# Hymba-style decoder step: all turns of x ahead of the gate columns, the gate columns behind the second weight chunk, and the gate chain behind the scaled copies

## The chip, the cores and the metric

One core of one Trainium2 chip runs the whole step. The metric is the device time of one execution in microseconds, as the median of the runs shown. All data is float32.

## The reference, cut to what matters

256 prompt tokens and 8 sample tokens (264 columns in all) of width 2048 go through one layer: a mixing half (RMSNorm, one combined input projection, mLSTM heads and sliding-window attention, output projection), a mixture of experts, a gated embedding and a final norm. The change lies in the first hundred microseconds, where this is computed:

```python
h = rmsnorm(x, g_mix)                       # x * rsqrt(mean(x^2) + eps) * g
mq, mk, mv, mo, mi, mf, aq, ak, av = split_in(h @ w_in)
i_pre = mi + b_i                            # input gate, one column a head
logf  = log_sigmoid(mf + b_f)               # forget gate, one column a head
F = cumsum(logf); a = i_pre - F; m_t = F + max(m0, cummax(a))
```

mi and mf are 4 columns each of h @ w_in (the gate columns). All the others are projected in groups of 512 columns. F, a and m_t are what the mLSTM stage needs of the gates.

## The kernel before

Every engine has an instruction stream of its own, written out by hand in the order in which it runs; semaphores join them. mix_project (L306) is the first stage. Its parts:

- **Loads.** SyncE's queue (SP) issues x into x_res in two halves of the 2048 columns (L370; turns 0 to 7 need the first, turns 8 to 15 the second), then four weight chunks of 1 MB (load_chunk, L143), each into a slot of its own in raw. A chunk is 512 weight rows by 512 columns; four chunks make a group. A chunk's successor in the same slot is loaded when TensorE has gone through it. Then SP loads chunk 4, waits for the running maximum of the gates (L377), stores it to DRAM and loads it back spread over all partitions (amax_wide, L380), and goes on with chunks 5 and up, and the first three mLSTM states. ScalarE's queue loads the rows of the gains (grows, L458) and the 8 gate columns of w_in (wg, L460), which are 2048 pieces of 32 bytes. GpSimd spreads wg into columns 0 to 3 and 32 to 35 of each block of wg8 (L354), and then raises n_zero.
- **TensorE.** It runs WARM = 14 matmuls on a constant tile (L415), turns the gain rows (L418), and then turns x (turn, L394): for each of 16 blocks k of 128 columns, three transposes into one of six PSUM banks. ScalarE (even k, L465) and VectorE (odd k, L503) copy a bank out, times the gain, to raw_h; turn k waits for the copy of turn k - 6. From turn 4 on each turn is followed by a gate column matmul for block k - 4 (gate_columns, L407: stationary 36 columns of wg8, moving 264 columns of raw_h; a float32 matmul is two instructions in the trace). TensorE waits for n_zero between turn 3 and turn 4 (L422). Then come chunk 0 of group 0 on raw_h (project_chunk, L153, matmul at L160), a broadcast of the inverse root of the mean square (L432), chunk 1, a wait for the gate chain (L435) with small transposes of its results (L439 to L443), chunk 2, a small matmul for the sample decays (L446), and chunk 3. Groups 1 and 2 (chunks 4 to 11) use hT, which is raw_h times the inverse root.
- **ScalarE.** After its copies it sums the squares of two of the three tiles (L469), takes the root (L475), the exponentials and the logarithm of the gate chain (L477 to L485), eight exponentials of the decay matrix (L490), and copies the banks of groups 1 and 2.
- **VectorE.** After its copies it sums the squares of tile 1 (L506, L508), forms r_rows (L518, after n_zero, since core.ones is set before it), copies r_wide (L521), and runs the gate chain: gates, log sigmoid, two scans (L525 to L543), then copies of the small transposes and the sample decays (L545 to L559). Only then come the 16 scaled copies raw_h times r_wide to hT (L564), the decay matrix et from amax_wide (L569, L570), and the copies of group 0's banks times r_wide (L577).

After this stage come attention, mLSTM, the output projection, norm and router (norm_stage, whose 48 transposes are L265), 32 experts with 192 weight loads of 2048 KB, and the tail. Each begins when the one before it has ended on its engines; SP issues the first expert weights at L1476, after the norm.

Of the kernel before, what the change touches and what calls it, by code (L numbers as in the profile page):

```python
# [25 lines left out]
ALU = mybir.AluOpType  # L26
ACT = mybir.ActivationFunctionType
AX = mybir.AxisListType.X

P = 128  # L30
D = 2048
KD = D // P
SEQ, NS = 256, 8
NT = SEQ + NS
TILES = ((0, P), (P, P), (SEQ, NS))
MH, DK = 4, 256
# [20 lines left out]
C_SLOTS = 3  # L57
WARM = 14
NONE = 4096.0
# [121 lines left out]
def bank_done(core, engine, g, j):  # L181

    engine.wait_ge(core.proj_done, 4 * g + j + 1)
# [122 lines left out]
def mix_project(core, w, hT, mixT, pT, m, ctx):  # L306
# [11 lines left out]
    wg = S("wg", [P, KD, 2 * MH])  # L318
    warm = S("warm", [P, 256])
    squares = S("norm_squares", [P, D])  # L320
# [10 lines left out]
    et, cols, col, sg, tab, mend = m["et"], m["cols"], m["col"], m["sg"], m["tab"], m["mend"]  # L331
    names = ("n_consts n_zero n_warm n_x0 n_x1 n_grows n_gcolsT n_gcols n_wg n_turned n_copied_act n_copied_dve n_squares n_square1 "
             "n_mean n_root n_rows n_wideT n_wide n_scaled gates_done m_small m_causal m_lf1 m_lf2 m_arow m_en m_colsT m_cols m_sT m_sg1 m_sg2 m_diag m_tabT "
# [5 lines left out]
    with nc.Block() as block:  # L339
        @block.gpsimd  # L340
        def _(pool):
            link = chain(pool, core.pool_chain)
            nc.gpsimd.memset(warm[:], 1.0).then_inc(q["n_warm"], 1)
            link(nc.gpsimd.memset(core.ident[:], 0.0))
            link(nc.gpsimd.affine_select(out=core.ident[:], in_=core.ident[:], compare_op=ALU.not_equal,
                                         fill=1.0, base=0, pattern=[[-1, P]], channel_multiplier=1))
            link(nc.gpsimd.memset(r[:], 1.0))
            pool.sem_inc(q["n_consts"], 1)
            link(nc.gpsimd.memset(wg8[:], 0.0))
            link(nc.gpsimd.memset(core.ones[:], 1.0))  # L350
            link(nc.gpsimd.memset(core.eps[:], EPS))
            pool.wait_ge(q["n_wg"], 16)
            for b in range(2):
                link(nc.gpsimd.tensor_copy(wg8[:, :, 32 * b:32 * b + MH], wg[:, :, b * MH:(b + 1) * MH]))  # L354
            pool.sem_inc(q["n_zero"], 1)
            link(nc.gpsimd.affine_select(out=core.upper[:], in_=core.ones[:], compare_op=ALU.is_gt,
                                         fill=0.0, base=0, pattern=[[1, P]], channel_multiplier=-1))
            link(nc.gpsimd.memset(causal[:], 0.0))

            link(nc.gpsimd.affine_select(out=causal[:], in_=causal[:], compare_op=ALU.is_ge, fill=-BIG,  # L360
                                         base=0, pattern=[[1, 256]], channel_multiplier=-1))
            pool.sem_inc(q["m_causal"], 1)

        @block.sync
        def _(sp):
# [5 lines left out]
            for n in range(NCH):  # L371
# [3 lines left out]
            sp.dma_start(sg[:, 0, :], w["state_mlstm_m"][0]).then_inc(q["m_small"], 16)  # L375
            load_chunk(core, sp, NCH)
            sp.wait_ge(q["m_arow"], 1)  # L377
            sp.dma_start(core.amax_rows, amax[:]).then_inc(q["m_amax"], 16)
            sp.wait_ge(q["m_amax"], 16)
            sp.dma_start(amax_wide[:].rearrange("p h t -> p (h t)"),  # L380
                         core.amax_rows.rearrange("(o h) t -> o (h t)", o=1).to_broadcast([P, MH * SEQ])
                         ).then_inc(q["m_amax"], 16)
            for n in range(NCH + 1, after + NCH):
                load_chunk(core, sp, n)
                if n == NCH + 1:
                    sp.wait_ge(q["n_squares"], 1)
                    sp.wait_ge(q["n_square1"], 1)
                    sp.wait_ge(q["gates_done"], 1)
                if n - NCH - 1 < C_SLOTS:
                    load_state(core, sp, w, m["cst"], n - NCH - 1)  # L390

        @block.tensor
        def _(pe):
# [12 lines left out]

            def gate_columns(k):  # L407

                pe.wait_ge(q[("n_copied_act", "n_copied_dve")[k % 2]], k // 2 + 1)
                return nc.tensor.matmul(ps[0:32 + MH, 6, 0:NT], wg8[:, k, :], raw_h[:, k, :],  # L410
                                        start=(k == 0), stop=(k == KD - 1))

            pe.wait_ge(q["n_warm"], 1)
# [5 lines left out]
            pe.wait_ge(q["n_x0"], 48)  # L419
            for k in range(4):  # L420
                turn(k)
            pe.wait_ge(q["n_zero"], 1)  # L422
            for k in range(4, KD):
                turn(k)
                gate_columns(k - 4)
            for k in range(KD - 4, KD):
                last = gate_columns(k)
            last.then_inc(q["gates_done"], 1)
            project_chunk(core, pe, raw_h, 0)
            pe.wait_ge(q["n_rows"], 1)  # L430
            for t, (t0, n) in enumerate(TILES):
                last = nc.tensor.matmul(ps[:, 7, t0:t0 + n], r_rows[0:n, t, :], core.ident[0:n, 0:n], start=True, stop=True)  # L432
            last.then_inc(q["n_wideT"], 1)
            project_chunk(core, pe, raw_h, 1)
            pe.wait_ge(q["m_arow"], 3)  # L435
            for kind in range(3):
                for b in range(2):
# [5 lines left out]
            nc.tensor.transpose(ps[0:NS, 7, MH:2 * MH], lf[:, SEQ:NT], core.ident[0:MH, 0:MH]).then_inc(q["m_sT"], 1)  # L443
            project_chunk(core, pe, raw_h, 2)
            pe.wait_ge(q["m_diag"], 1)
            nc.tensor.matmul(ps[:, 6, 0:64], core.ones[0:NS, :], diag[:].rearrange("p a b h -> p (a b h)"),  # L446
                             start=True, stop=True).then_inc(q["m_tabT"], 1)
            project_chunk(core, pe, raw_h, 3)
            for n in range(NCH, after):
                if n == NCH:  # L450
                    pe.wait_ge(q["n_scaled"], KD)
                project_chunk(core, pe, hT, n)

        @block.scalar
        def _(act):
            at = 0
            for name, n in (("g_mix", 16), ("g_mh", 8), ("g_ffn", 16), ("g_ple", 16)):
                act.dma_start(core.grows[at:at + n, :], w[name].rearrange("l (k p) -> (l k) p", p=P)).then_inc(q["n_grows"], 16)  # L458
                at += n
            act.dma_start(wg[:], w["w_in"][0].rearrange("(k p) c -> p k c", p=P)[:, :, C_GATES:C_GATES + 2 * MH]  # L460
                          ).then_inc(q["n_wg"], 16)
            act.wait_ge(q["n_gcols"], 1)
            for k in range(0, KD, 2):
# [31 lines left out]
        def _(dve):  # L495
# [19 lines left out]
            link(V.reciprocal(r[:], r[:]))  # L515
            dve.wait_ge(q["n_zero"], 1)
            for t in range(3):
                ins = V.tensor_scalar(r_rows[:, t, :], core.ones[:], r[:, t:t + 1], None, ALU.mult)  # L518
            ins.then_inc(q["n_rows"], 1)
            dve.wait_ge(q["n_wideT"], 1)  # L520
            link(V.tensor_copy(r_wide[:], ps[:, 7, 0:NT]))  # L521
            dve.wait_ge(q["gates_done"], 1)
            for b in range(2):
# [38 lines left out]

            for k in range(KD):
                V.tensor_tensor(hT[:, k, :], raw_h[:, k, :], r_wide[:], ALU.mult).then_inc(q["n_scaled"], 1)  # L564

            dve.wait_ge(q["m_causal"], 1)
# [6 lines left out]
            link(V.tensor_copy(tab[:, 0:2].rearrange("p a b h -> p (a b h)"), ps[:, 6, 0:64]))  # L573
            for j in range(4):

                bank_done(core, dve, 0, j)
                V.tensor_tensor(pT[:, GROUP_TILES[0] + j, :], ps[:, j, 0:NT], r_wide[:], ALU.mult).then_inc(core.copied["V"], 1)  # L577
            for g in range(1, A_GROUPS):
# [1696 lines left out]
```

## Time and profile before

| | us |
|---|---|
| median of 3 runs (lowest to highest) | 1798.15 (1793.78 to 1799.5) |
| the profiled execution | 1802.88 |
| its span | 1801.2 |
| TensorE busy, weight loads busy | 1413.7 (78%), 809.0 (45%) |
| VectorE, ScalarE, GpSimd busy | 264.1, 305.4, 101.4 |

The span runs from the first to the last instruction of the core. The profile cuts it into 40 slices of 45 us and shows for each how busy an engine was and which clock TensorE was granted (in tenths of full speed), and it lists who waited for whom. Times of instructions are counted from the span's start.

### The profile page before, as it was taken

The numbers are of one execution on the slowest core, as the hardware profiler recorded it, in microseconds if no ns is written. First come the engines' busy times: TensorE is split into PE (matmuls) and PEld (weight loads), VectorE is DVE, ScalarE is ACT, GpSimd is POOL, SyncE is SP. The second block draws the span as 40 slices with busy tenths as digits, with TensorE's granted clock in tenths as the row PEclk, the third lists the DMA queues.
The fourth block names the chain that finished last, engine by engine and source line by source line (L and its number), as shares of the span: only waits on it lengthen the run. The fifth ranks groups of instructions, "written<-read, shape, count | busy, mean of one in ns | idle before, by whom it ended". The sixth has DMA issues, their size and how long they took to land. (4 is left out here: it accounts for less than half of the span.)

```text
span 1801.2 us, 21059 instructions
## 1 busy us (share of the span) xinstructions
PE 1413.7 (78%) x8611; PEld 809.0 (45%) x8612; DVE 264.1 (15%) x725; ACT 305.4 (17%) x560; POOL 101.4 (6%) x190
## 2 busy tenths in 40 slices
PE   7999999999996657666676767677676767676997
PEld 3787888888885532222222222222222222223553
DVE  1402220046514210000000000000000000001312
ACT  1202121132201001111111111111111111112303
POOL 0000000010000011010101010101000010100000
PEclk6999998999998558888878787878777787878999
DMA  4547342469751829999999999999999999973532
GB/s 144 178 160 217 117 127 89 139 252 332 256 213 44 307 99 428 428 426 427 427 428 428 427 427 428 426 423 415 423 412 416 425 412 426 417 323 116 196 135 101
DMA packets 108772, 541.01 MB, mean 300 GB/s; under 512 B 15032, under 2 KB 37756, under 8 KB 82077
## 3 DMA queue, kind: packets, MB, share of 16 engines
q1 hardware_dynamic: 101348, 531.58, 74.3%
q0 software_dynamic: 5200, 8.67, 1.3%
q8 instruction: 34, 0.56, 0.1%
q10 hardware_dynamic: 2176, 0.09, 0.1%
q14 instruction: 14, 0.11, 0.0%
HBM read 523.99 MB, written 24.62 MB: 305 GB/s over the span
## 5 line engine op out<-in xcount | busy, mean ns | idle before, releaser
L1758 PE MATMUL ps<-raw,xT_slots 128*32 128x512 f32 x1536 | 245.0, 770 | 198.7 <-DMA raw<-in_w_gate 95.8
L160 PE MATMUL ps<-hT,raw 128*128 128x264 f32 x1280 | 295.0, 391 | 0.0
L160 PEld LDWEIGHTS ps<-hT,raw 128*128 128x128 f32 x1280 | 243.8, 192 | 43.2 <-issue 1.3
L1778 PE MATMUL ps<-more,hid 128*32 128x512 f32 x1024 | 179.3, 837 | 63.5 <-DMA more<-in_w_down 49.4
L1758 PEld LDWEIGHTS ps<-raw,xT_slots 128*32 128x32 f32 x1536 | 46.8, 123 | 349.3 <-DMA raw<-in_w_up 130.0
L160 PE MATMUL ps<-mixT,raw 128*128 128x264 f32 x640 | 147.4, 391 | 1.2 <-PEq L927 1.2
L1767 PEld LDWEIGHTS ps<-fold,gu 128*128 128x128 f32 x512 | 83.2, 244 | 112.1 <-ACT gu L1679 62.3
L160 PEld LDWEIGHTS ps<-mixT,raw 128*128 128x128 f32 x640 | 122.2, 192 | 23.0 <-issue 2.0
L1991 PE MATMUL ps<-raw,gate_xT 128*128 128x512 f32 x256 | 113.5, 600 | 0.3 <-DMA raw<-in_w_ple_gate 0.3
L1778 PEld LDWEIGHTS ps<-more,hid 128*32 128x32 f32 x1024 | 34.2, 131 | 176.7 <-DMA more<-in_w_down 86.9
L1728 DVE TENSOR_TENSOR hid<-ps,sig 128x128 f32<-128x128 f32 x32 | 9.3, 291 | 699.3 <-PE ps L1767 699.3
L1767 PE MATMUL ps<-fold,gu 128*128 128x32 f32 x512 | 90.7, 328 | 23.1 <-ACT gu L1679 23.1
L1758 PE MATMUL ps<-more,xT_slots 128*32 128x512 f32 x512 | 88.6, 829 | 9.2 <-DMA more<-in_w_up 8.3
L1749 PEld LDWEIGHTS ps<-ident,xe 128*64 128x64 f32 x1056 | 66.3, 216 | 39.2 <-issue 39.2
L1682 ACT ACTIVATE xT_slots<-ps 128x512 f32<-128x512 f32 x32 | 19.1, 597 | 349.3 <-PE ps L1749 336.7
L1749 PE MATMUL ps<-ident,xe 128*64 128x64 f32 x1056 | 70.9, 289 | 5.7 <-DMA xe<-ffn_rows,gi 5.7
L1991 PEld LDWEIGHTS ps<-raw,gate_xT 128*128 128x128 f32 x256 | 48.3, 192 | 57.9 <-issue 57.4
L1852 POOL DMA_INDIRECT expert_rows<-yq,si x32 | 32.9, 1028 | 697.2 <-DVE yq L1736 697.2
L1736 DVE COPY yq<-ps 128x512 f32<-128x512 f32 x32 | 22.1, 691 | 227.2 <-PE ps L1778 227.2
L1673 ACT ACTIVATE gu<-ps 128x512 f32<-128x512 f32 x32 | 19.1, 597 | 200.8 <-PE ps L1758 200.8
L1676 ACT ACT_TABLE_LOAD x32 | 41.1, 1283 | 0.6
L1673 ACT ACT_TABLE_LOAD x32 | 41.1, 1283 | 0.5
(383 smaller groups left out, 892.5 us busy)
## 6 DMA issues: line engine op xcount, KB each, us to landing
raw<-in_w_gate SPq DMA_DIRECT2D x64, 2048.0 KB
more<-in_w_down SPq DMA_DIRECT2D x64, 2048.0 KB, 28.6
raw<-in_w_up SPq DMA_DIRECT2D x32, 2048.0 KB
more<-in_w_up SPq DMA_DIRECT2D x32, 2048.0 KB
raw<-in_w_in SPq DMA_DIRECT2D x44, 1024.0 KB, 5.1
raw<-in_w_out SPq DMA_DIRECT2D x16, 1024.0 KB, 5.9
raw<-in_w_ple_gate SPq DMA_DIRECT2D x16, 1024.0 KB, 5.1
x_res<-in_state_mlstm_C SPq DMA_DIRECT2D x8, 1024.0 KB, 9.6
```

Of the source, the lines that this page charges most:

```text
L160: return nc.tensor.matmul(ps[:, j, 0:NT], core.raw[:, q % NCH, k * GW + j * P:k * GW + (j + 1) * P], xT[:, core.groups[g].k0 + c * CK + k, ...
L1673: nc.scalar.activation(gu[:, 0, :], ps[:, GATE, :], ACT.Copy).then_inc(q["gu_copied"], 1)
L1676: nc.scalar.activation(sig[:], ps[:, GB, 0:4 * SLOTS].rearrange("p (k s) -> p k s", k=4), ACT.Sigmoid).then_inc(q["sig_ready"], 1)
L1682: nc.scalar.activation(xT[:], ps[:, XB, :].rearrange("p (k s) -> p k s", k=EK), ACT.Copy).then_inc(q["x_copied"], 1)
L1728: V.tensor_tensor(hid[:], ps[:, GB, 0:4 * SLOTS].rearrange("p (k s) -> p k s", k=4), sig[:], ALU.mult).then_inc(q["h_step"], 1)
L1736: V.tensor_copy(yq[:], ps[:, YB, :]).then_inc(q["y_copied"], 1)
L1749: last = nc.tensor.matmul(ps[h * 64:(h + 1) * 64, XB, k * 64:(k + 1) * 64], by_row[:, k, :], quarters[:, h], start=True, stop=True)
L1758: last = nc.tensor.matmul(ps[own, (GATE, UP)[m], :], xT[:, k, i * SLOTS:(i + 1) * SLOTS], chunk(m * EI + i)[:, k * GW:(k + 1) * GW], start ...
L1767: last = nc.tensor.matmul(ps[:, GB, (m * 4 + j) * SLOTS:(m * 4 + j + 1) * SLOTS], gu[:, m, :].rearrange("p (i r k) -> p i k r", i=EI, k=2) ...
L1778: last = nc.tensor.matmul(ps[a * SLOTS:(a + 1) * SLOTS, YB, :], hid[:, 2 * i + k, :], chunk(2 * EI + i)[:, k * D + a * GW:k * D + (a + 1) ...
L1852: pool.indirect_dma_start(out=y4, out_offset=bass.IndirectOffsetOnAxis(ap=si[:, 0:1], axis=0), in_=yq[:], in_offset=None, bounds_check=8 * ...
L1991: last = nc.tensor.matmul(ps[:, 2 * t + g % 2, :], xT[:, c * CK + k, t * P:(t + 1) * P], core.raw[:, c, k * GW:(k + 1) * GW], start=(c == ...
```

## The change

- TensorE: 9 warm-up matmuls in place of 14. All 16 turns in one row, without a wait for n_zero and without gate columns between them. One wait for all copies, then chunks 0 and 1, the broadcast of the inverse root, and only then n_zero and the 16 gate column matmuls. Chunks 2 and 3, chunks 4 to 6, the small transposes (with their wait for m_arow), chunk 7, the small matmul of the decays (with its wait for m_diag), and chunks 8 to 11 follow.
- VectorE: r_rows waits for n_ones, raised right behind the memset of core.ones, and no more for n_zero. The scaled copies to hT, and the copies of group 0's banks, stand ahead of the gate chain.
- SP: chunks 4 and up are loaded as slots come free, without a wait between them; the store of amax stands behind the issue of chunk 8, its spread load behind the issue of chunk 9. The states are loaded with chunks 4, 5 and 6.
- ScalarE: one tiny activation (L460 and following) as soon as the warm-up tile is set.

```diff
-WARM = 14
+WARM = 9
@@ gpsimd
             link(nc.gpsimd.memset(core.ones[:], 1.0))
+            pool.sem_inc(q["n_ones"], 1)
@@ sync
-            load_chunk(core, sp, NCH)
-            sp.wait_ge(q["m_arow"], 1)
-            sp.dma_start(core.amax_rows, amax[:]).then_inc(q["m_amax"], 16)
-            sp.wait_ge(q["m_amax"], 16)
-            sp.dma_start(amax_wide[:]...).then_inc(q["m_amax"], 16)
-            for n in range(NCH + 1, after + NCH):
+            for n in range(NCH, after + NCH):
                 load_chunk(core, sp, n)
-                if n == NCH + 1:
+                if n == NCH:
+                    sp.wait_ge(q["n_turned"], KD)
                     sp.wait_ge(q["n_squares"], 1)
                     sp.wait_ge(q["n_square1"], 1)
-                    sp.wait_ge(q["gates_done"], 1)
-                if n - NCH - 1 < C_SLOTS:
-                    load_state(core, sp, w, m["cst"], n - NCH - 1)
+                if n - NCH < C_SLOTS:
+                    load_state(core, sp, w, m["cst"], n - NCH)
+                if n == NCH + 4:
+                    sp.wait_ge(q["m_arow"], 1)
+                    sp.dma_start(core.amax_rows, amax[:]).then_inc(q["m_amax"], 16)
+                if n == NCH + 5:
+                    sp.wait_ge(q["m_amax"], 16)
+                    sp.dma_start(amax_wide[:]...).then_inc(q["m_amax"], 16)
@@ tensor
-            for k in range(4):
+            for k in range(KD):
                 turn(k)
-            pe.wait_ge(q["n_zero"], 1)
-            for k in range(4, KD):
-                turn(k)
-                gate_columns(k - 4)
-            for k in range(KD - 4, KD):
-                last = gate_columns(k)
-            last.then_inc(q["gates_done"], 1)
+            pe.wait_ge(q["n_copied_act"], KD // 2)
+            pe.wait_ge(q["n_copied_dve"], KD // 2)
             project_chunk(core, pe, raw_h, 0)
+            project_chunk(core, pe, raw_h, 1)
             pe.wait_ge(q["n_rows"], 1)
             ...
             last.then_inc(q["n_wideT"], 1)
-            project_chunk(core, pe, raw_h, 1)
+            pe.wait_ge(q["n_zero"], 1)
+            for k in range(KD):
+                last = nc.tensor.matmul(ps[0:32 + MH, 6, 0:NT], wg8[:, k, :], raw_h[:, k, :], start=(k == 0), stop=(k == KD - 1))
+            last.then_inc(q["gates_done"], 1)
+            project_chunk(core, pe, raw_h, 2)
+            project_chunk(core, pe, raw_h, 3)
+            pe.wait_ge(q["n_scaled"], KD)
+            for n in range(NCH, NCH + 3):
+                project_chunk(core, pe, hT, n)
             pe.wait_ge(q["m_arow"], 3)
             ...
-            project_chunk(core, pe, raw_h, 2)
+            project_chunk(core, pe, hT, NCH + 3)
             pe.wait_ge(q["m_diag"], 1)
             ...
-            project_chunk(core, pe, raw_h, 3)
-            for n in range(NCH, after):
-                if n == NCH:
-                    pe.wait_ge(q["n_scaled"], KD)
+            for n in range(NCH + 4, after):
                 project_chunk(core, pe, hT, n)
@@ scalar
+            act.wait_ge(q["n_warm"], 1)
+            nc.scalar.activation(first_use[:], warm[:, 0:1], ACT.Copy)
             act.wait_ge(q["n_gcols"], 1)
@@ vector
-            dve.wait_ge(q["n_zero"], 1)
+            dve.wait_ge(q["n_ones"], 1)
             ...
             link(V.tensor_copy(r_wide[:], ps[:, 7, 0:NT]))
+            for k in range(KD):
+                V.tensor_tensor(hT[:, k, :], raw_h[:, k, :], r_wide[:], ALU.mult).then_inc(q["n_scaled"], 1)
+            for j in range(4):
+                bank_done(core, dve, 0, j)
+                V.tensor_tensor(pT[:, GROUP_TILES[0] + j, :], ps[:, j, 0:NT], r_wide[:], ALU.mult).then_inc(core.copied["V"], 1)
             dve.wait_ge(q["gates_done"], 1)
             ...
-            for k in range(KD):
-                V.tensor_tensor(hT[:, k, :], raw_h[:, k, :], r_wide[:], ALU.mult).then_inc(q["n_scaled"], 1)
             ...
             link(V.tensor_copy(tab[:, 0:2].rearrange("p a b h -> p (a b h)"), ps[:, 6, 0:64]))
-            for j in range(4):
-                bank_done(core, dve, 0, j)
-                V.tensor_tensor(pT[:, GROUP_TILES[0] + j, :], ps[:, j, 0:NT], r_wide[:], ALU.mult).then_inc(core.copied["V"], 1)
```

## Rows read from the trace of the kernel before

**Rows 1.** The page's 40 slices of 45 us: DMA share in tenths.

```profile
DMA  4547342469751829999999999999999999973532
```

**Rows 2.** Stretches: length, busy PE, PEld, DVE, ACT, POOL, clock, DMA share, GB/s.

```profile
7.50:10.90 3.40, 3.40 (x19) 2.25 (x17) 0.71 (x2) 1.18 (x1) 0.00 (x0) 1.00 1.05 357
22.40:45.00 22.60, 22.56 (x62) 8.39 (x63) 3.78 (x7) 5.54 (x9) 1.00 (x3) 0.50 0.00 1
65.50:68.90 3.40, 3.40 (x10) 2.58 (x9) 2.91 (x11) 0.21 (x1) 0.00 (x0) 0.50 0.89 296
580.00:593.20 13.20, 13.18 (x48) 7.43 (x48) 3.03 (x7) 3.12 (x8) 0.00 (x0) 0.50 0.43 164
660.00:1600.00 940.00, 651.65 (x4512) 239.90 (x4512) 39.48 (x93) 145.55 (x188) 77.13 (x126) 0.80 1.00 419
```

**Rows 3.** Timelines of VectorE and ScalarE, and one issue of SP, 9 to 600 us.

```profile
11.24 0.49 DVE L503 TENSOR_SCALAR mixT<-ps,gcols 128x264 f32<-128x264 f32 x1 [0.48 <-PE ps L403]
55.27 0.88 DVE L525 TENSOR_TENSOR gates<-ps,norm_r_wide 4x264 f32<-4x264 f32 x2
63.31 0.28 DVE L543 TENSOR_SCALAR arow<-arow 4x256 f32<-4x256 f32 x1
66.57 5.58 DVE L564 TENSOR_TENSOR hT<-mixT,norm_r_wide 128x264 f32<-128x264 f32 x16
...
9.72 1.28 ACT L465 ACT_TABLE_LOAD   x1 [9.60 <-PE ps L403]
42.22 1.90 ACT L469 ACTIVATE norm_squares<-x_res 128x2048 f32<-128x2048 f32 x1
72.85 2.87 ACT L490 ACTIVATE gain_row<-gain_row,cols 128x256 f32<-128x256 f32 x8 [7.04 <-DVE gain_row L570]
...
598.64 0.94 SPq L1476 DMA_DIRECT2D raw<-in_w_gate x2
```

**Rows 4.** Timeline of TensorE, 0 to 140 us: start, length, line, operation, idle time before.

```profile
1.20 7.71 PE L415 MATMUL ps<-warm 128*128 128x256 f32 x28 [1.20 <-POOL warm L343]
...
9.04 2.16 PE L403 MATMUL ps<-ident,x_res 128*128 128x128 f32 x12
22.44 0.89 PE L403 MATMUL ps<-ident,x_res 128*128 128x128 f32 x3 [11.24 <-POOLq L355]
...
24.29 0.89 PE L403 MATMUL ps<-ident,x_res 128*128 128x128 f32 x3
...
43.58 3.11 PE L410 MATMUL ps<-mixT,wg 128*36 128x264 f32 x10
46.62 7.39 PE L160 MATMUL ps<-mixT,raw 128*128 128x264 f32 x32
53.84 0.92 PE L432 MATMUL ps<-ident,norm_r_rows 128*128 128x128 f32 x6
54.69 7.39 PE L160 MATMUL ps<-mixT,raw 128*128 128x264 f32 x32
63.64 0.53 PE L439 MATMUL ps<-ident,arow 4*128 4x4 f32 x6 [1.56 <-DVE arow L543]
...
64.15 9.07 PE L160 MATMUL ps<-mixT,raw 128*128 128x264 f32 x32
73.16 0.43 PE L446 MATMUL ps<-diag,ones 8*128 8x64 f32 x2
73.52 7.39 PE L160 MATMUL ps<-mixT,raw 128*128 128x264 f32 x32
80.74 57.12 PE L160 MATMUL ps<-hT,raw 128*128 128x264 f32 x256
```

**Rows 5.** Longest waits of GpSimd, 0 to 60 us: total, times, longest.

```profile
POOL wg L354 <- DMA wg<-in_w_in: 18.7, 1, 18.7
```

**Rows 6.** DMA issues in 3.4 to 3.5 us (chunk 0): us to landing last.

```profile
raw<-in_w_in SPq DMA_DIRECT2D x1, 1024.0 KB, 10.5
```

More of the change, by code:

```diff
@@ L318, in mix_project @@
     wg = S("wg", [P, KD, 2 * MH])
-    warm = S("warm", [P, 256])
+    warm, first_use = S("warm", [P, 256]), S("first_use", [P, 1])
     squares = S("norm_squares", [P, D])
@@ L331, in mix_project @@
     et, cols, col, sg, tab, mend = m["et"], m["cols"], m["col"], m["sg"], m["tab"], m["mend"]
-    names = ("n_consts n_zero n_warm n_x0 n_x1 n_grows n_gcolsT n_gcols n_wg n_turned n_copied_act n_copied_dve n_squares n_square1 "
+    names = ("n_consts n_ones n_zero n_warm n_x0 n_x1 n_grows n_gcolsT n_gcols n_wg n_turned n_copied_act n_copied_dve n_squares n_square1 "
              "n_mean n_root n_rows n_wideT n_wide n_scaled gates_done m_small m_causal m_lf1 m_lf2 m_arow m_en m_colsT m_cols m_sT m_sg1 m_sg2 m_diag m_tabT "
@@ L375, in _ @@
             sp.dma_start(sg[:, 0, :], w["state_mlstm_m"][0]).then_inc(q["m_small"], 16)
-            load_chunk(core, sp, NCH)
-            sp.wait_ge(q["m_arow"], 1)
-            sp.dma_start(core.amax_rows, amax[:]).then_inc(q["m_amax"], 16)
-            sp.wait_ge(q["m_amax"], 16)
-            sp.dma_start(amax_wide[:].rearrange("p h t -> p (h t)"),
-                         core.amax_rows.rearrange("(o h) t -> o (h t)", o=1).to_broadcast([P, MH * SEQ])
-                         ).then_inc(q["m_amax"], 16)
-            for n in range(NCH + 1, after + NCH):
+            for n in range(NCH, after + NCH):
                 load_chunk(core, sp, n)
-                if n == NCH + 1:
+                if n == NCH:
+                    sp.wait_ge(q["n_turned"], KD)
                     sp.wait_ge(q["n_squares"], 1)
                     sp.wait_ge(q["n_square1"], 1)
-                    sp.wait_ge(q["gates_done"], 1)
-                if n - NCH - 1 < C_SLOTS:
-                    load_state(core, sp, w, m["cst"], n - NCH - 1)
+                if n - NCH < C_SLOTS:
[5 more added lines that the diff above has]
+                    sp.wait_ge(q["m_amax"], 16)
+                    sp.dma_start(amax_wide[:].rearrange("p h t -> p (h t)"),
+                                 core.amax_rows.rearrange("(o h) t -> o (h t)", o=1).to_broadcast([P, MH * SEQ])
+                                 ).then_inc(q["m_amax"], 16)
         @block.tensor
@@ L405, in turn @@
                 last.then_inc(q["n_turned"], 1)
[L407 to L411, printed above, removed]
             pe.wait_ge(q["n_warm"], 1)
```

## The prediction

> **What bounds the kernel now.** I read the page's slices first. The DMA digits stand at 9 from about 660 us to 1600 us and below that before it [rows 1]: in that stretch the queues run at 419 GB/s with a share of 1.00, and TensorE is busy 652 of 940 us [rows 2]. So the expert stage is bound by its weights. But its first weights are issued at 598.6 us, by an SP that arrives there only when norm and router begin [rows 3]; nothing in it is tied to a fixed time. What comes before is bound by TensorE: from 80.74 us eight chunks follow each other in 57.12 us, 7.14 us each, without a gap [rows 4]. A microsecond saved ahead of chunk 4 should therefore move everything behind it, up to the end.
>
> The timeline of TensorE shows where the first 80 us go [rows 4]. Warm-ups end at 8.9 us; four turns follow in 2.16 us; then TensorE is idle for 11.24 us. The releaser named is GpSimd, and GpSimd itself waited 18.7 us for the 32-byte pieces of wg [rows 5]. When TensorE comes back at 22.44 us its clock is 0.50, that is 1.2 GHz, and stays so to 45 us although it is busy 22.56 of 22.60 us [rows 2]. One turn and one gate column matmul take 24.29 - 22.44 = 1.85 us there. Chunk 0 begins at 46.62 us. Chunks 0 and 1 take 7.2 us each, then TensorE waits 1.56 us for the gate chain, the clock falls again at 65.5 us for 3.4 us, and chunk 2 takes 9.0 us where chunk 3 takes 7.2. **Chunk 4 begins at 80.74 us.** That number is what the change moves.
>
> **The change, part by part.** The sum is the new start of chunk 4.
>
> 1. *Start of the turns.* The second MB of a load behind another follows 3.0 us later at 353 to 357 GB/s (1.05 MB by 0.357) [rows 2]. Chunk 0 landed at 3.4 + 10.5 = 13.9 us [rows 6]; the second half of x, ahead of it, then at about 10.9, and the first at about 7.9. The gain rows had landed by 8.9 us, where TensorE waited for nothing [rows 4]; when, no row shows. Nine warm-ups end between 6.1 and 6.7 us (28 instructions in 7.71 us, at 0.275 us each or less for the ten removed). So the transposes of the gain rows start between 7.9 and 8.9 us; I take 8.2, and the first turn at 8.4. The second half of x is needed by turn 8, which comes after 12.5 us: its wait costs nothing, and at worst (x landing with chunk 0 at 13.9) 1.4 us less what the slower clock already takes.
>
> 2. *Sixteen turns.* At 2.4 GHz four turns took 2.16 us with the tail of the last, 0.52 us each from start to start. At 1.2 GHz the 48 transposes of the later norm took 13.19 us, 0.82 us a turn [rows 2]. There the clock was 0.50 for all 13 us with TensorE busy all the time: turns alone did not bring it up. Whether they let it fall is not shown. From 7.5 to 10.9 us it was kept, with 1.4 us of warm-ups and the four turns in it [rows 2]; in 62 to 65.5 us about as much matmul work, without turns, did not keep it. In the changed kernel the warm-ups are over at 6.7, then comes an idle 1.5 us, then turns alone. I take it that the clock falls near 10.9 us. Then 4.8 turns run in 2.5 us and 11.2 at 0.82 us, 9.2 us: the turns end at 20.1 us. The bounds are 16 x 0.52 = 8.3 us (end at 16.7) and 16 x 0.82 = 13.2 us (end at 21.6). The rotation through six banks costs nothing: a copy takes 0.49 us [rows 3], each engine has one per two turns (1.04 us or more). The early tiny activation takes a table load (1.28 us [rows 3]) out of the way of the first copy; turn 6 is 3 us behind turn 0 and covers it either way: zero, and up to 1.3 us where it did not. The last copy and its hand-over add 0.7 us: **chunk 0 starts at 20.8 us.** Both its load and that of chunk 1 (3.0 us later, 16.9 us) are in.
>
> The Trainium skill ("TensorE: Matmul & The Clock Gate", Part 4, PE-mode transpose) says that the full clock doesn't engage in transpose mode. By that rule all sixteen turns would run at 1.2 GHz and end at 21.6 us in place of 20.1, and 18.8 us would be saved in place of 20.3; the later norm agrees (0.50 throughout), the four turns at 9.04 us, still at the full clock, do not.
>
> 3. *The slow start of chunk 0.* The clock came back at 45.0 us only 1.4 us into unmixed matmuls, and in the second case at 68.9 us, 4.8 us after chunk 2 began. I take 3.4 us at half clock, as in 65.5 to 68.9, which costs 1.7 us (chunk 2's excess over chunk 3 was 1.7); bounds 0.7 and 2.4, half of the two times named.
>
> 4. *The work up to chunk 4.* Four chunks at 7.22 us (46.62 to 53.84) are 28.9; the broadcast of the inverse root is 54.69 - 53.84 = 0.85; sixteen gate column matmuls are 32 instructions with 264 moving columns, which at the full clock go at the chunks' rate (32 in 7.22 us): 7.2 us. The bound above is that of the last ten in the trace, 43.58 to 46.62, 0.30 each over a changing clock: 9.7 us. The small transposes and the decay matmul (0.51 and 0.36 us) now come after chunk 4's start; I add 0.9 so that the comparison is fair.
>
> **Sum:** 20.8 + 1.7 + 28.9 + 0.85 + 7.2 + 0.9 = 60.4 us against 80.74. **20.3 us are saved.**
>
> **What is hidden, and by what.** TensorE's wait for r_rows: the squares begin with the last copy; from their start at 42.22 us to the broadcast at 53.84, which had no idle time ahead, are 11.6 us at most; two chunks of 14.4 us cover it. n_zero came at 22.4 us and is asked for after 37 us; gone with the wait is the whole 11.24 us. r_wide and the sixteen scaled copies (5.58 us) run beside gate columns and chunk 2: 21.7 us of cover. Group 0's bank copies follow the banks, as before. The gate chain then starts behind them, at the end of chunk 3, and takes what it took from 55.27 to 63.59, 8.3 us [rows 3], some 9 us with the last bank copy; TensorE asks for it after three chunks, 21.4 us later. The SP wait for m_arow has the loads of chunks 9 to 11 behind it: it ends about 7.5 us into the group, when chunk 8's slot has just come free; a load is needed 21 us after it can start and takes 5 or so. The next things late would be at the change from group 1 to group 2: VectorE needs the transposes (after chunk 6) and then does the decays (from 63.59, the transposes' 0.5 us among it, to 66.57, so 2.5 us without them) and et; ScalarE's eight exponentials run in step with et and end 3.6 us after it began (72.15 to 75.72); its first bank copy must be there when chunk 8 starts. Transposes at 21.9 us of the group, decays at 24.4, exponentials at 28.0, copy (0.4) at 28.4, chunk 8 at 29.5. That cover is **1.1 us only**, and each microsecond more is lost one for one.
>
> **The rivals.**
> A. *Forecast: the clock falls in the turns, 20.3 us saved.* Own range 18.0 (all turns slow and the latest rise) to 22. Chance 0.62.
> B. *The clock holds through the turns.* They end at 16.7, chunk 0 starts at 17.4 at the full clock: 17.4 + 28.9 + 0.85 + 7.2 + 0.9 = 55.3, saved 25.5, in the run's terms 1772.7 us. For it: it was kept from 7.5 to 10.9 us with turns in it. Against: the later norm. Chance 0.18.
> C. *A new wait at the group change.* amax's spread load stands behind chunk 9's load; with its issue at 14.7 us of the group and a landing as long as chunk 0's 10.5 us it would be there at 25.2, 0.8 us after VectorE asks for it; if it takes twice that, et is 11 us late and TensorE loses 10 of the 20 us: saved 10 to 19, 1779 to 1788 us. Against: by then one load of 1 MB stands ahead of it, where chunk 0 had the whole of x ahead. Chance 0.12.
> D. *No gain at the end*, some later stage waiting for something not moved by the stage before: 1798 us. Against it speaks that the loads of experts are issued when SP gets there [rows 3]. Chance 0.04.
> E. *Slower: the clock stays at 1.2 GHz* beyond the turns, through chunks 0 to 3 and the gate columns, whose stationary side is 36 columns. That work is 37 us at 2.4 GHz and twice that at 1.2: 35.3 us more than forecast, 15 us slower than before, 1813 us. It decides from 44 us of low clock on (half of which eats 20.3 + 1.7 us). Against: both times the clock came back within 5 us of dense matmuls [rows 2, 4]. Chance 0.04.
>
> **The numbers.** The profiled execution took 1802.9 us (span 1801.2): 1782.6 after. The median of the runs is 4.7 us lower, 1798.15: **1777.9 us**. Runs of this kernel spread over 5.7 us, so 0.3% (5.4 us) is about what can be told from no change. Range: B's 1772.7 less 2.5 for that spread, 1770, and on the other side the bounds of A with the gate columns at 9.7 us (1783) and the nearer half of C, 1785. Faster by over 0.3% are A, B and C: 0.92. Within: D, 0.04. Slower: E, 0.04.
>
> **What would show it.** Right: no idle time behind turn 3; turns of 0.52 us up to about 11 us and of 0.82 after; chunk 0 at 20 to 22 us; a granted clock of 0.50 ending up to 5 us into it; gate columns in one row of 7.2 us near 38 us; no wait at L435, L446 or at chunk 8; router and experts earlier by the same 20 us. Wrong: turns with waits for copies or for x; a clock of 1.00 from 4 us on (B); a wait of TensorE for ScalarE's copy at chunk 8 (C); a shift that shrinks between chunk 4 and 660 us (D); a clock of 0.50 past 30 us (E).

## The result, and the profile after

| | before | after |
|---|---|---|
| median of the runs shown (lowest to highest) | 1798.83 (1793.78 to 1803.05), 4 runs | 1778.22 (1776.4 to 1782.85), 4 runs |
| the profiled execution, its span | 1802.88, 1801.2 | 1778.48, 1776.8 |

The ratio is 0.9885, 95% interval 0.9866 to 0.9905: 17 to 24 us faster. The forecast was 1777.9. Six more runs of the changed kernel beside eleven of the kernel before gave 0.9891 (0.9871 to 0.9910), 1778.72 against 1800.44. Intervals in brackets behind a ratio are 95% intervals, here and below. The number was met; the road to it was not the one forecast, as the traces show.

The page's DMA slices of the changed kernel, which answer to [rows 1]: the row of nines, 20 slices long, is the same in kind; a slice is now 44.4 us where it was 45.0.

```profile
DMA  7564432679632759999999999999999999974542
```

TensorE's timeline of the changed kernel, 0 to 114 us, to be held against [rows 4] (start, length, line and operation, idle time before):

```profile
1.20 6.93 PE L411 MATMUL ps<-warm 128*128 128x256 f32 x18 [1.20 <-POOL warm L343]
8.80 0.24 PE L414 MATMUL ps<-ident,grows 56*128 56x56 f32 x1 [0.67 <-DMA grows<-in_g_ple]
8.97 8.44 PE L405 MATMUL ps<-ident,x_res 128*128 128x128 f32 x48
18.04 14.48 PE L160 MATMUL ps<-mixT,raw 128*128 128x264 f32 x64 [0.63 <-ACT mixT L464]
32.35 0.92 PE L424 MATMUL ps<-ident,norm_r_rows 128*128 128x128 f32 x6
33.20 7.31 PE L428 MATMUL ps<-mixT,wg 128*36 128x264 f32 x32
40.44 14.51 PE L160 MATMUL ps<-mixT,raw 128*128 128x264 f32 x64
54.79 21.52 PE L160 MATMUL ps<-hT,raw 128*128 128x264 f32 x96
76.24 0.53 PE L439 MATMUL ps<-ident,arow 4*128 4x4 f32 x6
...
76.75 7.39 PE L160 MATMUL ps<-hT,raw 128*128 128x264 f32 x32
84.07 0.43 PE L446 MATMUL ps<-diag,ones 8*128 8x64 f32 x2
84.43 28.75 PE L160 MATMUL ps<-hT,raw 128*128 128x264 f32 x128
```

The 11.24 us of idle time behind turn 3 are gone; the sixteen turns stand in one row of 8.44 us. Chunks 0 and 1, the broadcast, the gate columns and chunks 2 and 3 follow without a gap. There is no idle time ahead of L439 or of L446. Chunk 4 begins at 54.79 us where it began at 80.74: 25.95 us, of which 0.87 us (transposes and decay matmul, now behind it) is only moved. Most of it lies in the turns and gate columns: they took 37.58 us (9.04 to 46.62) and now take 9.07 and 7.24, which is 21.3 us less, 11.24 of it idle time and some 10 slow clock. The wait for the gate chain gives 1.56 and the slow chunk 2 behind it 1.8; the rest is the moved 0.87 and small gaps. The stretch of the turns, with the clock in the third column from the end:

```profile
9.00:17.40 8.40, 8.40 (x49) 5.32 (x48) 3.67 (x8) 3.84 (x9) 0.00 (x0) 1.00 1.09 358
17.40:45.00 27.60, 26.97 (x124) 20.42 (x123) 10.27 (x28) 6.67 (x8) 1.48 (x5) 1.00 0.62 204
```

The clock stays at 1.00 through the turns and behind them (it had risen at 6.85 us, among the warm-ups), where it stood at 0.50 from 22.4 to 45 us [rows 2].

**How a microsecond of the head reaches the end.** I read four moments in every trace: the first matmul on hT (chunk 4), the first transpose of the later norm, SP's first load of expert weights, and the end of the span.

| kernel | chunk 4 | norm | expert weights | span | from weights to end |
|---|---|---|---|---|---|
| before | 80.74 | 580.02 | 598.64 | 1801.2 | 1202.6 |
| before, second trace | 79.42 | 576.62 | 595.56 | 1797.7 | 1202.1 |
| after | 54.79 | 555.47 | 573.96 | 1776.8 | 1202.8 |
| after, second trace | 54.74 | 555.50 | 574.30 | 1776.5 | 1202.2 |
| after, third trace | 55.89 | 554.66 | 573.18 | 1775.9 | 1202.7 |

From the expert weights on, the time is the same to within 0.7 us in these five, and SP's issue moves with the stage ahead of it:

```profile
573.96 0.94 SPq L1474 DMA_DIRECT2D raw<-in_w_gate x2
```

So what is won ahead of chunk 4 is kept: 25.95 us there, 24.55 at the norm (0.87 of the difference is the moved work, the other 0.5 I did not place), 24.4 at the end.

### The profile page after: what moved, and what is told of

The parts are those of the page before. It is cut to its first block and busy times, and to the rows that moved or that the text cites. A ratio compares the mean times of both kernels' runs of the same rounds, so it can differ in the third digit from the quotient of the medians.

```text
span 1776.8 us, 21041 instructions
## 1 busy us (share of the span) xinstructions
PE 1420.2 (80%) x8601; PEld 808.4 (45%) x8602; DVE 264.9 (15%) x725; ACT 305.5 (17%) x561; POOL 101.4 (6%) x190
## 5 line engine op out<-in xcount | busy, mean ns | idle before, releaser
L1756 PE MATMUL ps<-raw,xT_slots 128*32 128x512 f32 x1536 | 256.8, 803 | 198.6 <-DMA raw<-in_w_gate 110.1
L1776 PE MATMUL ps<-more,hid 128*32 128x512 f32 x1024 | 170.7, 798 | 42.0 <-DVE hid L1729 20.5
L1756 PE MATMUL ps<-more,xT_slots 128*32 128x512 f32 x512 | 103.0, 952 | 11.4 <-DMA more<-in_w_up 11.1
L1756 PEld LDWEIGHTS ps<-more,xT_slots 128*32 128x32 f32 x512 | 18.3, 152 | 53.9 <-issue 39.1
```

The costliest lines, as they stand in the source:

```text
L1756: last = nc.tensor.matmul(ps[own, (GATE, UP)[m], :], xT[:, k, i * SLOTS:(i + 1) * SLOTS], chunk(m * EI + i)[:, k * GW:(k + 1) * GW], start ...
L1776: last = nc.tensor.matmul(ps[a * SLOTS:(a + 1) * SLOTS, YB, :], hid[:, 2 * i + k, :], chunk(2 * EI + i)[:, k * D + a * GW:k * D + (a + 1) ...
```

## The experiments

The table's columns for the variants, with the median of their runs (one run where so marked):

| kernel | chunk 4 | norm | span | median | ratio to before |
|---|---|---|---|---|---|
| e2, 14 warm-ups | 56.75 | 555.83 | 1777.2 | 1781.65 | 0.9902 (0.9882 to 0.9921) |
| e3, no warm-up | 62.34 | 566.83 | 1787.3 | 1785.08 | 0.9917 (0.9898 to 0.9937) |
| e5, gate columns ahead of chunk 0 | 61.17 | 560.61 | 1782.4 | 1785.94 | 0.9932 (0.9906 to 0.9958) |
| e6, the turns' order alone | 65.63 | 564.77 | 1788.0 | 1787.64 | 0.9936 (0.9917 to 0.9954) |
| e7, gate chain ahead of the copies | 54.98 | 556.04 | 1780.0 | 1779.37 | 0.9893 (0.9860 to 0.9925) |
| e8, small transposes behind chunk 3 | 64.45 | 571.20 | 1792.0 | 1792.65 | 0.9950 (0.9931 to 0.9970) |
| e9, gaps closed | 52.92 | 554.46 | 1777.7 | 1778.43 | 0.9891 (0.9870 to 0.9911) |
| e10, turns done twice | 73.66 | 573.97 | 1796.6 | 1798.3 (one) | |

### Both kernels once more: e1, e11 and e4

No edit. I wanted to know whether the full clock in the turns was luck.

> The changed kernel once more, unchanged. Its first trace had the clock at 1.00 through all sixteen turns (8.44 us for 48 transposes) and chunk 4 at 54.79 us. Theory 1 (a full clock reached by the warm-ups is kept by turns alone, whatever the moment of the run): again 8.4 to 8.6 us for the 48 transposes, chunk 4 at 54.5 to 56, span 24 to 25 us under the kernel before's. Theory 2 (the forecast's: it depends on when in the execution the chip looks; the first trace was a lucky one): the clock falls to 0.50 among the turns, these take 10 to 13 us, chunk 4 comes at 58 to 61, and the median of many runs is some 20 us below the kernel before, with runs of both kinds some 5 us apart.

> The changed kernel unchanged, for a third trace. Its ten timed runs lie in two bunches, seven at 1776.4 to 1778.9 us and three at 1781.8 to 1783.0. If a fall of the clock makes the upper bunch, a run of it shows one that the first two traces did not have, 3.4 us or more long, somewhere before 560 us; if this run is of the lower bunch, its clock changes are those of the first two, 10.2 us at 266, 3.4 at 300 and 3.4 at 437 us.

> The kernel before once more, for a second trace: is its first 80 us the same each time? Theory 1: clock 0.50 from 14 to 18 us on until about 45, chunk 4 at 79.5 to 82 us, and the spread of its runs (9 us from lowest to highest) comes from the expert stage. Theory 2: chunk 4 moves by more than 3 us from one execution to the next with the moments at which the clock changes.

The second trace of the changed kernel repeats the first: 48 transposes in 8.44 us, chunk 4 at 54.74. The third has the turns at the full clock too, but then a fall. Its stretches, beginning with the turns, columns as above:

```profile
9.00:17.40 8.40, 7.86 (x46) 4.96 (x45) 3.95 (x9) 4.39 (x9) 0.00 (x0) 1.00 1.09 351
17.50:20.80 3.30, 3.30 (x8) 2.58 (x9) 2.42 (x5) 3.25 (x5) 0.00 (x0) 0.50 1.09 356
20.90:33.00 12.10, 12.10 (x56) 10.32 (x55) 1.21 (x5) 2.66 (x3) 1.48 (x5) 1.00 0.51 167
```

Its chunks 0 and 1 took 16.12 us (17.49 us to 33.45 from start to the next start, 15.96) where they took 14.3 in the first: 1.6 us, at 0.50 for some 3.4 us. That is the size of step 3 of the forecast, in one execution of three. The expectation on the two bunches of times was wrong: this run took 1777.63 us, in the lower bunch, and has the fall. What it lacks is a later fall that the first trace has at 437 us (the first line is of the first trace, the second of the third):

```profile
437.00:440.30 3.30, 3.30 (x9) 2.57 (x9) 2.70 (x15) 0.00 (x0) 0.00 (x0) 0.50 0.98 329
437.00:440.30 3.30, 2.90 (x13) 2.58 (x14) 3.30 (x19) 0.00 (x0) 0.00 (x0) 1.00 0.89 241
```

So its chunk 4 comes 1.1 us later than the first trace's and its norm 0.8 us earlier: a fall more in the head and one less behind it cancel in the total. The timed runs of e1 lay at 1777.5 to 1778.9 (four) and at 1781.8 and 1783.0; what separates them I can't say.

The kernel before: its second trace has the clock at 0.50 from 15 to 46 us like the first, but no fall at 65.5, so that chunk 4 comes 1.3 us earlier. It also has the clock at 1.00 in 459 to 466 us, where the first trace has a fall (461.4 to 464.7 us at 0.51). Of the 3.5 us between the two spans, 3.4 are there at the norm already. So theory 1 held for the head, but these two runs do not differ by the expert stage. The runs beside these spread from 1792 to 1804 us, more than the head explains.

### Does the warm-up carry the turns' clock: e2 and e3

```diff
-WARM = 9
+WARM = 14     # e2
+WARM = 0      # e3
```

> The changed kernel with 14 warm-up matmuls as before. In the first trace of the changed kernel 9 warm-ups ended at 8.13 us because the clock rose at 6.85 only, and the gain rows landed 0.67 us later. Theory 1: 14 of them end at 9 to 10.5 us (0.22 us an instruction at the full clock, 0.44 below it), so chunk 0 starts 0.2 to 1.7 us later and the span is up to 1.7 us longer: not told from no change against the changed kernel. Theory 2: the longer warm-up keeps the clock up for longer among the turns: chunk 4 up to 4 us earlier than in runs of the changed kernel whose clock falls, so a median 1 to 4 us lower.

> The changed kernel without any warm-up matmul, so that the clock has nothing but turns to rise by: prices the case on which the forecast rested. If turns alone do not raise the clock (the later norm's 48 transposes ran 13.2 us at 0.50): 48 transposes take 13.2 us, chunk 0 starts at 22 to 23 us with a half clock for another 2 to 5 us, chunk 4 at 60.5 to 62, 6 to 7 us behind the changed kernel's first trace, ratio to the kernel before 0.990 to 0.993. If they do raise it after all: 9 to 11 us for the turns and chunk 4 at 55 to 58.

TensorE's timeline of e3:

```profile
8.90 0.32 PE L414 MATMUL ps<-ident,grows 56*128 56x56 f32 x1 [8.90 <-DMA grows<-in_g_ple]
9.15 13.19 PE L405 MATMUL ps<-ident,x_res 128*128 128x128 f32 x48
22.98 17.09 PE L160 MATMUL ps<-mixT,raw 128*128 128x264 f32 x64 [0.63 <-issue]
```

Without warm-ups 48 transposes take 13.19 us, exactly what the later norm's took in 580 to 593.2 us [rows 2]: turns alone don't raise the clock. Chunks 0 and 1 then take 16.9 us in place of 14.3, and chunk 4 comes 7.6 us late, 0.3 us beyond what I had expected; the median is 6.4 us above the changed kernel's. A warning on the reading: the stretches of this trace give the clock as 1.00 for the turns.

```profile
9.10:22.30 13.20, 13.20 (x49) 7.46 (x48) 3.67 (x8) 4.10 (x9) 0.48 (x2) 1.00 1.03 329
```

The durations contradict that: 0.275 us a transpose in 13.2 us, against 0.176 in the changed kernel's 8.44. Ahead of the first change of clock in a trace the column isn't a measurement. The same goes for the first microseconds of all of them: 18 warm-up instructions took 6.93 us in the changed kernel, 0.39 each, and 28 took 7.71 in the kernel before, 0.28 each, so part of them ran at the lower clock.

e2 is no better than the changed kernel: 14 warm-ups ended at 9.17 us, the turns came 0.33 us later, and this trace too has a fall right behind the turns.

```profile
9.30:17.70 8.40, 8.40 (x49) 5.36 (x48) 3.66 (x8) 3.81 (x9) 0.00 (x0) 1.00 1.11 347
18.30:21.60 3.30, 3.23 (x8) 2.53 (x9) 2.51 (x5) 3.27 (x4) 0.00 (x0) 0.50 1.02 338
```

So five more warm-ups cost a third of a microsecond at the start and did not prevent the fall in this trace. The medians, 1781.65 and 1778.72, are 2.9 us apart with overlapping intervals.

### Are turns able to keep the clock at all: e10

```diff
-                for t, (t0, n) in enumerate(TILES):
+                for t, (t0, n) in 2 * list(enumerate(TILES)):
                     last = nc.tensor.transpose(ps[:, k % 6, t0:t0 + n], ...)
```

> The changed kernel with every transpose of every turn done twice (96 for 48, into the same places): do turns keep the full clock for as long as they last, or had the sixteen been too short for a fall? Theory 1 (turns keep it): 96 transposes take 16.8 to 17.0 us at 1.00 and chunk 4 comes at 63.1 to 63.5. Theory 2 (a fall that is only late): the clock is 0.50 for part of them, they take 18.5 to 25 us, chunk 4 comes at 65 to 73.

```profile
9.30:12.10 2.80, 2.80 (x17) 1.79 (x17) 0.71 (x2) 0.48 (x1) 0.00 (x0) 1.00 1.08 353
12.20:33.70 21.50, 21.50 (x80) 12.27 (x79) 2.95 (x6) 4.39 (x8) 1.49 (x5) 0.50 0.47 152
```

Theory 2, and early: the turns began at 9.22 us at the full clock, and 3 us later it was 0.50 and stayed so for the remaining 21.5 us of transposes (24.58 us for 96; chunk 4 at 73.66, 0.7 beyond the expected range). This is the forecast's case A, in a kernel whose first 3 us of TensorE are those of the changed kernel but for the repeats and a longer wait for the gain rows. So turns neither raise the clock nor hold it safely. In all eight other traces in which sixteen turns ran in one row from a full clock, it was kept to the last of them, and in e9's, where the gain rows stand between them, too. The loss is one trace of one execution, and what decides between losing and keeping it I did not isolate; in the trace that lost it, TensorE had idled 1.69 us ahead of the turns, but in e8 it had idled 1.46 us and the clock was kept.

### How much is the turns' order alone: e6 and e5

e6 is the kernel before with this edit and no other:

```diff
-            for k in range(4):
+            for k in range(KD):
                 turn(k)
             pe.wait_ge(q["n_zero"], 1)
-            for k in range(4, KD):
-                turn(k)
-                gate_columns(k - 4)
-            for k in range(KD - 4, KD):
+            for k in range(KD):
                 last = gate_columns(k)
```

e5 is the changed kernel with the wait for n_zero and the gate columns moved up, between the wait for the copies and chunk 0.

> The kernel before with one thing changed: TensorE does all sixteen turns in a row, then waits for n_zero and does the sixteen gate column matmuls, then chunk 0 and all the rest as before (14 warm-ups, gate chain ahead of the scaled copies, wait for the gate chain behind chunk 1). Turns at 0.52 us end near 18 us; the gate columns start at 22.4 and end at 31 to 36 us by the clock; from chunk 0 to chunk 4 it is 32.4 to 34.1 us as in the two traces of the kernel before. Theory 1: chunk 4 at 64 to 70 us, 11 to 16 us of the some 25 gained, ratio 0.991 to 0.994; the rest is the placing behind chunk 1. Rival (the clock falls in the turns where the gate columns are next): 48 transposes in 10 us or more, chunk 4 at 68 to 72.

> The changed kernel, with the sixteen gate column matmuls and their wait for n_zero put between the turns and chunk 0: all else as changed. The turns end at 17.4 us, n_zero comes at 22.4. Theory 1 (the gain has two parts, turns ahead of the wait and the gate columns behind other work): TensorE idles 4.5 to 5 us behind the turns, the clock falls in or after that, the gate columns take 9 to 14 us in place of 7.2, chunk 4 comes at 61 to 66 us in place of 54.8, and 6 to 11 us of the gain are lost: ratio to the kernel before 0.992 to 0.996. Rival (only the order of the turns matters, since the clock is kept through 5 us of idle time): chunk 4 at 59.5 to 60, at most 5 us lost.

TensorE's timeline of e6:

```profile
9.93 8.44 PE L403 MATMUL ps<-ident,x_res 128*128 128x128 f32 x48
22.29 9.30 PE L410 MATMUL ps<-mixT,wg 128*36 128x264 f32 x32 [3.92 <-POOLq L355]
31.52 7.39 PE L160 MATMUL ps<-mixT,raw 128*128 128x264 f32 x32
...
48.54 0.53 PE L436 MATMUL ps<-ident,arow 4*128 4x4 f32 x6 [1.55 <-DVE arow L540]
...
49.04 9.07 PE L160 MATMUL ps<-mixT,raw 128*128 128x264 f32 x32
...
65.63 29.53 PE L160 MATMUL ps<-hT,raw 128*128 128x264 f32 x132
```

The order of the turns alone moves chunk 4 from 80.74 to 65.63 us: 15.1 of the 25.95 us. It takes the turns out of the wait and out of the low clock, as theory 1 had it. Its turns also began 0.96 us later than the changed kernel's. Three costs remain: 3.92 us of idle time for n_zero, the gate columns slowed to 9.2 us, and the wait for the gate chain with the fall of the clock behind it (1.55 and 1.8 us, chunk 2 taking 9.0 us as before). e5's timeline shows the first two by themselves:

```profile
8.93 8.44 PE L405 MATMUL ps<-ident,x_res 128*128 128x128 f32 x48
22.77 8.93 PE L422 MATMUL ps<-mixT,wg 128*36 128x264 f32 x32 [5.40 <-POOLq L356]
31.63 14.51 PE L160 MATMUL ps<-mixT,raw 128*128 128x264 f32 x64
```

5.40 us idle, less the 0.63 that it has in the changed kernel, and 8.86 in place of 7.24 us for the gate columns (22.77 to 31.63) make 6.4 us, and chunk 4 comes at 61.17, 6.4 us late. That is theory 1, near its lower edge: the loss is above the rival's 5 us, 4.8 us of it idle time and 1.6 us the clock, which stood at 0.50 for the first 3.3 us of the gate columns and at 1.00 after. The median lost 7.2.

### The order on VectorE, and the distance of the small transposes: e7 and e8

e7 puts VectorE's scaled copies and the bank copies of group 0 behind the gate chain's last m_arow; e8 puts TensorE's wait for m_arow and the small transposes from behind chunk 6 to right behind chunk 3.

> The changed kernel with VectorE's gate chain (up to the third m_arow) ahead of the sixteen scaled copies and the four bank copies, as in the kernel before. Gate columns are done at 40.4 us, the chain takes 8.3, the scaled copies 5.6: hT is whole at 54.4 us, and TensorE asks for it at 54.8. Theory 1 (this part only orders what is hidden anyway): chunk 4 waits at most 0.5 us, the time is that of the changed kernel to within 1 us. Rival (the reordering of VectorE carries part of the gain): TensorE waits 1 us or more at chunk 4 or at its second and third bank, and the clock falls there.

> The changed kernel with TensorE's wait for the gate chain and the small transposes right behind chunk 3 in place of behind chunk 6. The chain starts at 55.3 us and ends at 63.6, so TensorE idles 8.9 us there. Theory 1 (three chunks on TensorE hide the chain, and each microsecond without them is lost one for one): wait of 8.5 to 9.2 us at L439, the clock falls in it, chunk 4 at 64.1, slow for up to 5 us; 9 to 12 us of the gain lost, ratio 0.994 to 0.996. Rival (a later stage gives the time back): less than 6 us lost at the end.

VectorE's timeline in e7:

```profile
48.60 0.28 DVE L542 TENSOR_SCALAR arow<-arow 4x256 f32<-4x256 f32 x1
48.81 5.57 DVE L544 TENSOR_TENSOR hT<-mixT,norm_r_wide 128x264 f32<-128x264 f32 x16
54.40 1.45 DVE L548 TENSOR_TENSOR pT<-ps,norm_r_wide 128x264 f32<-128x264 f32 x4
```

hT is whole at 54.4 us, the copies of group 0 are late, and chunk 4 comes at 54.98, 0.2 us late, as theory 1 had it. The third headline of the change, the gate chain behind the scaled copies, is worth that and no more; it orders what is hidden either way once the gate columns are done at 40.4 us.

In e8 TensorE waits for the chain:

```profile
63.67 0.80 PE L436 MATMUL ps<-ident,arow 4*128 4x4 f32 x6 [8.74 <-DVE arow L548]
```

Chunk 4 comes 9.66 us late, as expected. But the norm comes 15.7 us late and the median is 13.9 us up, above what I had expected (9 to 12). The stretches of its trace show where the rest is:

```profile
59.90:70.00 10.10, 6.33 (x21) 5.01 (x22) 5.10 (x21) 1.44 (x4) 0.00 (x0) 0.50 0.00 1
128.10:134.90 6.80, 6.29 (x20) 4.96 (x21) 2.30 (x7) 0.76 (x4) 0.22 (x1) 0.50 0.85 241
```

The wait let the clock fall, and it stayed at 0.50 for 5.6 us into the chunks (2.8 us lost); a second fall of 6.8 us in the attention stage cost up to 3.4 more. A third, which lasts 10.2 us from 266 us on in the changed kernel's traces, lasts 13.6 here (278.1 to 291.7 us, clock 0.51), which costs up to 1.7. The first follows from the wait. The other two have no cause in it that I can show. e3 lost more than its head too (chunk 4 7.6 us late, the norm 11.4), and its trace has the same two: 6.7 us at 0.50 from 123.8 us, and 13.5 from 274.

### A version with the gaps closed: e9

```diff
-            pe.wait_ge(q["n_grows"], 64)
-            nc.tensor.transpose(ps[:, 7, 0:56], core.grows[:], ...)
             pe.wait_ge(q["n_x0"], 48)
             for k in range(KD):
+                if k == 2:
+                    pe.wait_ge(q["n_grows"], 64)
+                    nc.tensor.transpose(ps[:, 7, 0:56], core.grows[:], ...)
                 turn(k)
-            pe.wait_ge(q["n_copied_act"], KD // 2)
-            pe.wait_ge(q["n_copied_dve"], KD // 2)
-            project_chunk(core, pe, raw_h, 0)
+            for j in range(4):      # chunk 0, bank j behind the copy of turn 12 + j
+                pe.wait_ge(q[("n_copied_act", "n_copied_dve")[j % 2]], (12 + j) // 2 + 1)
+                ...
```

> A further step, from what the traces of the changed kernel show: TensorE waits 0.6 to 1.5 us for the gain rows at 8.75 us and 0.63 us for the last copy at 17.4, and in one trace the clock fell right behind the last turn. Here the gain rows are turned behind turn 1, and chunk 0 waits bank by bank (bank 0 for the copy of turn 12, bank 1 for that of turn 13, and so on), not for all copies. If both gaps are pure waiting: no idle time at chunk 0, chunk 4 at 53.3 to 54.4 us in place of 54.8, and no fall of the clock behind the turns; median 0.5 to 1.5 us below the changed kernel's 1778.7, which is not to be told apart from it by the runs, only by the trace. Rival: x itself lands no earlier than the gain rows, so that only the second gap closes (chunk 4 at 54.1 or later).

```profile
7.46 1.09 PE L405 MATMUL ps<-ident,x_res 128*128 128x128 f32 x6
8.62 0.26 PE L417 MATMUL ps<-ident,grows 56*128 56x56 f32 x1
8.82 7.39 PE L405 MATMUL ps<-ident,x_res 128*128 128x128 f32 x42
16.14 7.39 PE L423 MATMUL ps<-mixT,raw 128*128 128x264 f32 x32
```

Both gaps are closed: the turns begin at 7.46 us, so x had landed well ahead of the gain rows, and chunk 0 begins at 16.14 with no idle time. Chunk 4 comes at 52.92 us, 1.9 earlier, more than expected. The median is 1778.43, which the runs cannot tell from 1778.72. In this trace a fall of the clock at 115 us, in the attention stage, gave back part of it: the norm is only 1.0 us earlier. I count it as a shorter head, not as a faster kernel.

## Why the prediction was right, and where it was not

The total was right: 20.3 us forecast, 20.6 by the medians, 21.7 in the larger set (0.9891, that is 16 to 23 us). The traces say more: 24.4 us between the first pair, and 23.0 between the mean spans of two traces of the kernel before (1799.45) and three after (1776.4). The steps:

- *Bound and carry-over: right.* Every trace moves the expert stage with the head; from the first weights to the end all thirteen traces took 1201.9 to 1205.1 us. The rival of a gain lost at the end falls.
- *Step 1, start of the turns: 8.4 forecast, 8.97 measured.* The gain rows were the last to land, at 8.8 us. The warm-ups ended at 8.13, not by 6.7, since more of them ran at the lower clock; that cost nothing. x, put at 7.9, was there by 7.46 in e9.
- *Step 2, the turns: this step failed.* "I take it that the clock falls near 10.9 us" made 11.7 us of them. They took 8.44 us in all three traces of the changed kernel: rival B's 8.3, to which I had given 0.18. The evidence I leaned on, the later norm at 0.50, began at the low clock and shows that turns do not raise it (e3: 13.19 us again); it does not show that they let it fall. The Trainium skill ("TensorE: Matmul & The Clock Gate", Part 4, PE-mode transpose) says that the full clock doesn't engage in transpose mode; the 13.19 us of e3 agree with it and the changed kernel's 8.44 us do not. e10 shows a fall within turns, at 12.1 us, so case A can happen, but it did not in the sixteen turns here.
- *Step 3, a slow chunk 0: 1.7 forecast; none in two traces, 1.6 in the third.* It came from a fall just behind the turns, not from one within them. Where the turns did run at 1.2 GHz, the bound of 2.4 was passed: chunks 0 and 1 took 16.93 us in e3 and 16.79 in e10, 2.6 and 2.5 more than 14.31.
- *Step 4: right.* 28.9 forecast for four chunks, 14.31 + 14.35 = 28.7 measured; gate columns 7.2 and 7.24; broadcast 0.85 and 0.85. Measured total with the moved 0.87: 55.7 us against 60.4 forecast and 55.3 by rival B.
- *What is hidden: right.* No wait for n_zero, n_scaled, m_arow or m_diag. The thin cover at the change of groups was forecast as 1.1 us (copy at 28.4 us of the group, chunk 8 at 29.5). ScalarE's rows after, to be held against chunk 8 at 84.43:

```profile
80.02 2.88 ACT L489 ACTIVATE gain_row<-gain_row,cols 128x256 f32<-128x256 f32 x8 [1.61 <-DVE gain_row L572]
82.80 0.64 ACT L191 ACTIVATE pT<-ps 128x264 f32<-128x264 f32 x2
```

  Both copies are done at 83.44, 1.0 us ahead of chunk 8. Rival C fell: et began right behind the decays (79.23), so amax had landed.
- *Rival E fell:* the gate columns with their 36 columns ran 7.31 us at 1.00.
- *Parts without a run of their own.* The early activation and n_ones have no run of their own, but traces bound them. e6 has no early activation: its table load of 1.28 us stands at 10.61 us, ahead of ScalarE's first copy, and its 48 transposes took 8.44 us all the same. In the changed kernel GpSimd had spread wg by 22.3 us, and VectorE formed r_rows only at 23.09, behind the inverse root: the wait for n_zero would have cost nothing there. The new order of SP's loads is untested. In the changed kernel SP has m_arow at 62.5 us, so an SP that waited for it behind chunk 4's load, as before, would have issued chunk 5 only then, where TensorE begins it at about 62 us; I take the new order for a condition of the rest, but no run shows it.

So by the traces the head gained 4.7 us more than forecast, and the medians show 3 to 4 us less than the first pair of traces. That gap comes from the executions that were profiled. The forecast carried the 4.7 us between the profiled execution of the kernel before and its median over to the changed kernel. There the profiled execution (1778.48) lies only 0.3 us above the median, while the one before (1802.88) lies 4.1 us above its own in the table above: 24.4 less 3.8 is the 20.6 of the medians. Part of the 4.1 us can be seen: the first trace of the kernel before has two falls of the clock that its second has not. The rest of the scatter stays open (12 us before, 6.6 us after); the interval (16 to 23 us) holds the traces' mean difference of 23.0 only at its edge, and not the 24.4 of the first pair.

The hit was luck. By the forecast's own signs (a clock of 1.00 in the turns, chunk 0 at 18.04 us and not at 20 to 22) it was rival B that came true, and B's figure for the median, 1772.7, is 5.5 us below the measured 1778.2. Case A, whose mechanism did not act, came within 0.3 us, since the 4.7 us by which it put the turns and chunk 0 too high were nearly balanced by the 3.8 us above and by 0.7 us lost between chunk 4 and the end.

## What to carry to other kernels

Where an in-order engine waits for a slow small load in the middle of work that doesn't need it, put the work first and the consumer of the load behind enough of other work to cover both the load and the chain that follows it; the idle time returns, and with it what the clock lost in it (here 11.24 us of idle time had brought some 10 us of slow clock with it). Price a stretch by where its clock starts: the same 48 transposes were 8.44 us from a full clock and 13.19 from a low one. And after moving work behind a dependent chain, compute the cover at each point where the chain is asked for: three chunks covered it with 12 us to spare, none left 8.7 us of wait and a slow restart.

## What the runs showed of the hardware that I had not expected

- Sixteen turns that began at the full clock kept it for 8.44 us in every trace (three of the changed kernel, and e2, e5, e6, e7, e8), although turns never raised it; but twice as many transposes in e10 lost it after 3 us. The outcome is not fixed by the kernel's text alone: the third trace of the unchanged program had a fall that the first two did not.
- More warm-ups did not prevent a fall: with 14 of them (e2, one trace) one came right behind the turns all the same.
- The clock column reads 1.00 ahead of the first change of clock in a trace, even where the durations (0.275 us a transpose) are those of 1.2 GHz.
- Falls of 3.3 us and more turned up in the attention stage at 115, 124 and 128 us in traces whose code there is the same (e9, e3, e8), and not in the others. The fall of 3.4 us at 437 us in the changed kernel's first two traces is missing in its third, and that at 461 us in the kernel before is missing in its second. From chunk 4 to the norm this makes some 2 us (500.7 and 500.8 against 498.8 us; 499.3 against 497.2), with the same text, so single traces can't be told apart by less than that.
